# A two-part network on one core: transposed inputs, modulation in column tiles, and three projections woven among its sets

## What is computed

```python
mod = silu(c) @ w_ada[l] + b_ada[l]          # c: one vector of 1024; w_ada: 1024 x 3072
mod_c = silu(c_ctx) @ w_ada[l] + b_ada[l]
shift, scale, gate = split(mod, 3); shift_c, scale_c, gate_c = split(mod_c, 3)
h = rms_norm(x, norm_g[l]) * (1.0 + scale) + shift              # x: 512 x 1024
hc = rms_norm(ctx, norm_g[l]) * (1.0 + scale_c) + shift_c       # ctx: 256 x 1024
# then a = (h @ w_in[:, :512]) * sigmoid(h @ w_in[:, 512:1024]), a convolution over 31 taps, and the rest
```

## Time and profile before

| | |
|---|---|
| Time, median of 3 runs | 3198.05 us (3197.98 to 3198.81) |
| Profiled execution: span | 3200.0 us |
| TensorE busy | 3079.6 us, 96% |
| VectorE busy | 1861.0 us, 58% |
| ScalarE busy | 1308.2 us, 41% |
| GpSimd busy | 344.1 us, 11% |
| DMA | 251.53 MB, mean 79 GB/s |

### The profile page before, as it was taken

The page is one execution under the profiler, slowest core; times in us unless marked ns, Lnnn a source line. Parts: engine busy times, 40 slices in busy tenths (PEclk is TensorE's granted clock), DMA queues, the critical chain, the costliest instruction groups (busy, mean ns, idle before and its releaser), DMA issues.

```text
span 3200.0 us, 37158 instructions
## 1 busy us (share of the span) xinstructions
PE 3079.6 (96%) x14848; PEld 2424.0 (76%) x14848; DVE 1861.0 (58%) x2906; ACT 1308.2 (41%) x2017; POOL 344.1 (11%) x241
## 2 busy tenths in 40 slices
PE   8999999999999999999999999999999989999998
PEld 5877877877788676668667777788888866788887
DVE  5877695455435767673533786666535672466632
ACT  3345534244532344632444464322225567422222
POOL 0011131210000001101220020000003210000000
PEclk9999999999999999999999999999999999999999
DMA  5222132320012322223101232323332310223332
GB/s 209 67 66 73 47 115 77 109 84 26 21 34 76 106 83 74 65 85 101 40 30 50 88 96 80 99 92 94 98 95 89 116 37 1 73 93 94 97 93 73
DMA packets 78733, 251.53 MB, mean 79 GB/s; under 512 B 9120, under 2 KB 11168, under 8 KB 78560
## 3 DMA queue, kind: packets, MB, share of 16 engines
q1 hardware_dynamic: 72672, 227.91, 22.5%
q0 software_dynamic: 5024, 18.09, 1.8%
q10 hardware_dynamic: 864, 3.15, 0.2%
HBM read 247.01 MB, written 2.10 MB: 78 GB/s over the span
## 4 chain that ended last, share of the span: by engine, by line
PE 45%; DVE 3%; ACT 3%; issue 1%; DVEq 0%; ACTq 0%
PE PS L1145 31%; PE PS L1783 3%; PE PS L2800 3%; PE PS L2901 1%; PE PS L1907 1%; PE PS L2878 1%; PE PS L2879 1%; PE PS L2860 0%; PE PS L2861 0%; PE PS L2822 0%; ACT WH L1094 0%; PE PS L2531 0%; ACT L1970 0%; DVE PS L3049 0%; PE PS L2870 0%
## 5 line engine op out<-in xcount | busy, mean ns | idle before, releaser
L1104 DVE TENSOR_TENSOR WL<-RAW,WH 128x1024 fp32r<-128x1024 f32 (+2 forms) x372 | 432.3, 1163 | 513.0 <-ACT WH L1094 512.4
L1094 ACT ACTIVATE WH<-RAW 128x1024 fp32r<-128x1024 f32 (+4 forms) x425 | 407.5, 965 | 430.7 <-PE PS L1145 333.9
L1783 PE MATMUL PS<-Hh,WH 128*128 128x512 f32 x1376 | 516.1, 375 | 14.3 <-DVE WL L1104 6.5
L1783 PE MATMUL PS<-Hh,WL 128*128 128x512 f32 x1376 | 489.2, 356 | 0.0
L1783 PE MATMUL PS<-Hl,WH 128*128 128x512 f32 x1376 | 488.9, 355 | 0.0
L1783 PEld LDWEIGHTS PS<-Hh,WH 128*128 128x128 f32 x1376 | 260.9, 190 | 76.8 <-issue 23.3
L1145 PE MATMUL PS<-XH,WH 128*128 128x512 f32 x768 | 306.1, 399 | 0.0
L1145 PE MATMUL PS<-XH,WL 128*128 128x512 f32 x768 | 304.5, 396 | 0.0
L1145 PE MATMUL PS<-XL,WH 128*128 128x512 f32 x768 | 304.4, 396 | 0.0
L1783 PEld LDWEIGHTS PS<-Hl,WH 128*128 128x128 f32 x1376 | 260.6, 189 | 44.6 <-issue 7.2
L1783 PEld LDWEIGHTS PS<-Hh,WL 128*128 128x128 f32 x1376 | 261.5, 190 | 38.2
(11 more groups left out here) (404 smaller groups left out, 5759.4 us busy)
## 6 DMA issues: line engine op xcount, KB each, us to landing
RAW<-in_w_in SPq DMA_DIRECT2D x124, 512.0 KB, 3.6
RAW<-in_ffn_in SPq DMA_DIRECT2D x96, 512.0 KB, 3.5
RAW<-in_ffn_out SPq DMA_DIRECT2D x48, 512.0 KB, 3.5
RAW<-in_w_ada SPq DMA_DIRECT2D x32, 384.0 KB, 3.6
RAW<-in_nsa_in SPq DMA_DIRECT2D x21, 512.0 KB, 3.3
RAW<-in_lru_in SPq DMA_DIRECT2D x20, 512.0 KB, 3.5
MW<-in_w_ada SPq DMA_DIRECT2D x32, 256.0 KB, 9.6
BS<-in_bs POOLq DMA_DIRECT2D x16, 512.0 KB, 3.9
```

What stands on the lines that cost most here:

```text
L1094: act.activation(WH[half[j]][:, 0:n], RAW[j % NRAW][:, 0:n], ACT.Copy).then_inc(*did("act_whi", ("whi", j)))
L1104: dve.tensor_tensor(WL[half[j]][:, 0:n], RAW[j % NRAW][:, 0:n], WH[half[j]][:, 0:n].bitcast(F32), ALU.subtract).then_inc(*did("dve_wlo", ( ...
L1783: mm = pe.matmul(ps[:, c:c + w_], wt[:, 128 * k:128 * k + 128], x[:, a:a + w_], start=(k == 0 and q == 0), stop=(k == n - 1 and q == 2))
```

## The change

x and the context come transposed from memory in the layout of `X` and `XC2`, so that transposes, copies and `XT` go; they are loaded on SP's queue ahead of the constants. Squares are taken elementwise (ScalarE for x, VectorE for the context), summed over the partitions by full-precision matmuls with ones, and the root is taken on all 768 columns with the helper that later norms use (`act_rsqrt`, `dve_rsqrt`: two halves of 384 columns). A piece of the modulation becomes four matmuls of 128 columns, one into each group of 32 PSUM partitions (a set's 512 results then stand in 4 x 2 partitions by 128 columns, whose other partitions are cleared once), and its turn one matmul with 8 picked columns of the identity. Pieces 0 to 7 run before the first projection. The first three projections (`OPEN`) are opened together: for each set their blocks 2c and 2c+1, with the pieces of the next set between them and its turn at the end. Their weights are loaded early, and GpSimd makes the remainder for the third.

```diff
+AHEAD = ((0, 0), (0, 1), (1, 0))
+OPEN = (("cb", 0, 0), ("ca", 0, 0), ("cb", 0, 1))
 ...
         self.pairs.take("mod0")
-        self.pairs.take("modt0")
-        for i in range(6):
-            self.pairs.take(("x", i))
-            self.pairs.release(("x", i), ("x", i))
         self.pairs.take("roots0")
+        self.rsqrt("r0", "roots0")
+        self.win(("cb", 0, 0), 0, 512)
+        self.win(("ca", 0, 0), 0, 0)
+        self.win(("cb", 0, 1), 0, 640, 2)
         self.rms("in")
-        self.pairs.release("roots0", ("hx", "in", 7, 1))
-        self.pairs.release("mod0", ("row0", 2), ("row0", 3))
-        self.pairs.release("modt0", ("ab0", 2), ("ab0", 3))
+        self.tmp.release(("r0", "y"), ("hx", "in", 7, 0), ("hx", "in", 7, 1))
+        self.pairs.release("mod0", ("sh0", 3), ("ab0", 3), ("row0", 2), ("row0", 3))
 ...
         def sp_begin(sp):
             sp.dma_start(SMA[:, :], t["sm"][:, 0:SM_1]).then_inc(*did("q_sm", ("sm",), by=16))
+            for i in range(4):
+                sp.dma_start(X[:, 2 * i:2 * i + 2, :], t["x"][:, 2 * i:2 * i + 2, :]).then_inc(*did(f"q_x{i}", ("x0", i), by=16))
+            for i in range(2):
+                sp.dma_start(XC2[:, 4 * i:4 * i + 4, :], t["ctx"][:, 4 * i:4 * i + 4, :]).then_inc(*did(f"q_x{4 + i}", ("c0", i), by=16))
 ...
-                if i == 27:
-                    sp_loads(sp, 1)
+                if i == 7:
+                    sp_loads(sp, 2)
 
         def pool_begin(pool):
             pool.memset(EPSC[:, :], EPS).then_inc(*did("pool_set", ("eps",), ("turn", 0)))
+            pool_split(pool, [P.wj[("cb", 0, 1), 0]])
 ...
         def rows0(c):
-            return pairs.of("mod0")[:, 512 * (c % 2):512 * (c % 2) + 512]
+            return pairs.of("mod0")[:, 512 * (c % 2):512 * (c % 2) + 128]
 
         def turned0(c):
-            return pairs.of("modt0")[:, 512 * (c % 2):512 * (c % 2) + 8]
+            return pairs.of("mod0")[:, 512 * (c % 2) + 256:512 * (c % 2) + 264]
 
         def pe_begin(pe):
-            for i in range(6):
-                pe_turn(pe, i)
-                if 1 <= i < 5:
-                    pe_piece(pe, 2 * i - 2)
-                    pe_piece(pe, 2 * i - 1)
-            for i in range(8, 32):
+            ps = pairs.of("roots0")
+            for i in range(4):
+                for w in due("pe", ("sqx0", i), ("co",), pairs.after["roots0"]):
+                    pe.wait_ge(*w)
+                for k in (2 * i, 2 * i + 1):
+                    pe.matmul(ps[:, 0:S], ones, SQX[:, k, :], start=(k == 0), stop=(k == 7))
+            for i in range(2):
+                for w in due("pe", ("sqc0", i)):
+                    pe.wait_ge(*w)
+                for k in range(4 * i, 4 * i + 4):
+                    mm = pe.matmul(ps[:, S:NT], ones, SQC[:, k, :], start=(k == 0), stop=(k == 7))
+            mm.then_inc(*did("pe_sq", ("roots",)))
+            for i in range(8):
                 pe_piece(pe, i)
-                if i in (9, 17, 25):
-                    pe_turn0(pe, i // 8 - 1)
-                if i == 18:
-                    ps = pairs.of("roots0")
-                    for w in due("pe", ("dg",), ("co",), pairs.after["roots0"]):
-                        pe.wait_ge(*w)
-                    for a0, n, c in R768:
-                        mm = pe.matmul(ps[:, c:c + n], ones, DG[:, a0:a0 + n], start=True, stop=True)
-                    mm.then_inc(*did("pe_sq", ("roots",)))
-        def pe_turn(pe, i):
-            ps = pairs.of(("x", i))
-            for w in due("pe", ("xt", i), ("co",), pairs.after["x", i]):
+            pe_turn0(pe, 0)
+            for c in range(4):
+                n = 0
+                steps = [(name, k) for name in OPEN for k in (2 * c, 2 * c + 1)] if c in (0, 3) else [(name, k) for k in (2 * c, 2 * c + 1) for name in OPEN]
+                for name, k in steps:
+                    pe_open(pe, name, k)
+                    n += 1
+                    for i in PIECES[n] if c < 3 else ():
+                        pe_piece(pe, 8 * c + 8 + i)
+                if c < 3:
+                    pe_turn0(pe, c + 1)
+        PIECES = ((), (), (0,), (1, 2), (3, 4), (5, 6), (7,))
+        def pe_open(pe, name, k):
+            ps, j = pairs.of(name), P.wj[name, 0]
+            hi, lo = WH[half[j]], WL[half[j]]
+            xh, xl = hsrc(0)(k)
+            for w in due("pe", ("wlo", j), pairs.after[name], ("hl", "in", k)):
                 pe.wait_ge(*w)
-            for k in range(8):
-                mm = pe.transpose(ps[:, 128 * k:128 * k + 128], XT[i][:, 128 * k:128 * k + 128], ident)
-            mm.then_inc(*did("pe_x", ("xp", i)))
+            for a, n, c in R768:
+                for q, (wt, x) in enumerate(((hi, xh), (hi, xl), (lo, xh))):
+                    mm = pe.matmul(ps[:, c:c + n], wt[:, 128 * k:128 * k + 128], x[:, a:a + n], start=(k == 0 and q == 0), stop=(k == 7 and q == 2))
+            if k == 7:
+                mm.then_inc(*did("pe_lin", ("wfree", j), ("lin", name)))
 
         def pe_piece(pe, i):
             c, k = divmod(i, 8)
-            for w in due("pe", ("mw", i), ("cs",), ("row0", c - 2) if c >= 2 else pairs.after["mod0"]):
+            for w in due("pe", ("mw", i), ("cs",), ("row0", c - 2) if c >= 2 else [("mz",), pairs.after["mod0"]]):
                 pe.wait_ge(*w)
-            pe.matmul(rows0(c)[0:2, :], CS[:, 2 * k:2 * k + 2], MW[i % NMOD][:, :], start=(k == 0), stop=(k == 7)).then_inc(*did("pe_mod", ("mm0", i)))
+            for g in range(4):
+                mm = pe.matmul(rows0(c)[32 * g:32 * g + 2, :], CS[:, 2 * k:2 * k + 2], MW[i % NMOD][:, 128 * g:128 * g + 128], start=(k == 0), stop=(k == 7))
+            mm.then_inc(*did("pe_mod", ("mm0", i)))
 
         def pe_turn0(pe, c):
-            for w in due("pe", ("row0", c), ("co",), ("ab0", c - 2) if c >= 2 else pairs.after["modt0"]):
+            for w in due("pe", ("row0", c), ("co",), ("sh0", c - 2) if c >= 2 else None, ("ab0", c - 2) if c >= 2 else None):
 ...
+            pick = ident.rearrange("p (g n) -> p g n", g=4)[:, :, 0:2]
+            pe.matmul(turned0(c).rearrange("p (g q) -> p g q", g=4), ROW[:, c % 2, :], pick, start=True, stop=True).then_inc(*did("pe_modt", ("turn0", c)))
 ...
+            for i in range(4):
+                for w in due("act", ("x0", i)):
                     act.wait_ge(*w)
-                act.activation(XQ[:, :], XT[i][:, :], ACT.Square, accum_out=NM[:, i:i + 1]).then_inc(*did("act_sq", ("xsum", i)))
+                act.activation(SQX[:, 2 * i:2 * i + 2, :], X[:, 2 * i:2 * i + 2, :], ACT.Square).then_inc(*did("act_sq", ("sqx0", i)))
+            act_rsqrt(act, "r0", NT, load=False)
             act_row0(act, 0)
-            for w in due("act", ("root0", 0)):
-                act.wait_ge(*w)
-            act.activation(NM[:, 16:22], NM[:, 8:14], ACT.Ln).then_inc(*did("act_rs", ("root0", 1)))
-            for w in due("act", ("root0", 1)):
-                act.wait_ge(*w)
-            act.activation(NM[:, 16:22], NM[:, 16:22], ACT.Exp, scale=-0.5).then_inc(*did("act_rs", ("root0", 2)))
-            act_row0(act, 1)
-            act_rms(act, "in", HH[0], lambda k, q: MODS[0][:, k, q:q + 1], (2, 1))
+            act_split(act, 0)
+            act_high0(act, 0)
+            act_split(act, 1)
+            act_high0(act, 1)
+            act_split(act, 2)
+            for c in range(1, 4):
+                act_row0(act, c)
+                act_high0(act, 2 * c)
+                act_high0(act, 2 * c + 1)
 ...
+            for i in range(2):
+                for w in due("dve", pairs.after["mod0"]):
+                    dve.wait_ge(*w)
+                dve.memset(rows0(i), 0.0).then_inc(*did("dve_mz", ("mz",)))
 ...
+                xc = XC2[:, 4 * i:4 * i + 4, :]
+                dve.tensor_tensor(SQC[:, 4 * i:4 * i + 4, :], xc, xc, ALU.mult).then_inc(*did("dve_sq", ("sqc0", i)))
+            dve_rsqrt(dve, "r0", pairs.of("roots0"), NT, 1.0 / 1024, ("roots",))
             dve_turn0(dve, 0)
-            for w in due("dve", ("root0", 2)):
-                dve.wait_ge(*w)
-            dve.scalar_tensor_tensor(NM[:, 24:30], NM[:, 16:22], -0.5, NM[:, 16:22], ALU.mult, ALU.mult).then_inc(*did("dve_rs", ("root0", 3)))
-            for w in due("dve", ("root0", 3)):
-                dve.wait_ge(*w)
-            dve.tensor_tensor(NM[:, 24:30], NM[:, 24:30], NM[:, 8:14], ALU.mult).then_inc(*did("dve_rs", ("root0", 4)))
-            for w in due("dve", ("root0", 4)):
-                dve.wait_ge(*w)
-            dve.scalar_tensor_tensor(NM[:, 16:22], NM[:, 24:30], 1.5, NM[:, 16:22], ALU.add, ALU.mult).then_inc(*did("dve_rs", ("root0", 5)))
-            for i in range(6):
-                for w in due("dve", ("root0", 5), ("co",)):
-                    dve.wait_ge(*w)
-                dve.tensor_scalar(DG[:, 128 * i:128 * i + 128], ident, NM[:, 16 + i:17 + i], None, ALU.mult).then_inc(*did("dve_rs", ("dg",)))
-            dve_turn0(dve, 1)
```

(18 more changed lines are left out.)

97 lines of the change are left out of this document (43 added, 54 removed).

## The result

| | before | changed |
|---|---|---|
| Median of the runs | 3198.43 us | 3231.5 us (3226.03 to 3235.17) |
| Ratio to before | | 1.0092, 95% interval 1.0079 to 1.0105 |
| Span of the profiled execution | 3200.0 us | 3224.2 us |
| Repeated later, ratio to before | | 1.0097, 1.0083 to 1.0110 (r0_again) |

The sign and the range (3204 to 3235) were right; the 3219 of the forecast is 12.5 us too low, and it lies under every run.

The account below looks back on a forecast made before the run. TensorE was taken as the bound: third projection 18.1 us later (92.3 against 74.2) plus a 3.0 us norm stall made a span of 3221.1 us, less 2.0 for the median: 3219 us. Own range 3212 to 3227, wider range 3204 to 3235.

Parts of the forecast that it names:

- Start: Before the first projection: constants land at 12.7 us, sums ready at 24.6, first block at 34.8.
- The second block: Set 0: needs one more remainder and low part after the first block, so it starts at 37.0 us.
- costs nothing: GpSimd's remainder for the third projection: wanted only after several groups of set 0, so no time was counted.
- Set 0 behind its second block: First set from 37.0 us: five blocks 5.3 us and pieces 3.2, plus 0.9 for the clock.
- The 0.9 us of clock: TensorE at half clock after the wait before set 0, partly hidden by the second block's wait; bounds 0 and 2.7.
- The sets: First three projections: pieces 3.2 us a set, three TensorE waits of 4.8 us between sets, 2.0 us of clock each.
- Behind it: After the third projection: AP cleared late, VectorE's conv work late, a stall of 3.0 us at the first norm.
- Later VectorE has slack, and I count nothing: After the first norm: no further loss was counted for the rest of the program.
- The clock did not stay up: Rival at the waits before and between sets: full clock throughout, minus 6.9 us, 3212 us; chance 0.12.
- the constants did not overtake: Rival at the start: constants overtake the big loads, sums start 6 us earlier, 3213 us; chance 0.07.
- tiles ran side by side: Rival in the modulation pieces: tiles run serially, each piece 0.86 us, 3237 us; chance 0.08.
- the last rival: Between sets: modulation chain hidden behind a set's blocks, waits and their clock loss gone, 3199 us; chance 0.12.

Follow-up runs that it names:

- r0_again: The changed kernel unedited, measured once more as the control: 3232.8 us, ratio to before 1.0097.
- r1_turn_early: Changed kernel with all eight pieces of the next set behind a set's first block and the turn behind its second: 3203.97 us, ratio to before 1.0007.
- r10_vector_remainder: Changed kernel with the third projection's first remainder back on VectorE instead of GpSimd: 3228.49 us, ratio to before 1.0086.
- r2_clear_early: Changed kernel with GpSimd clearing AP behind the last turn, not behind the three projections: 3223.6 us.

## Why the prediction was right, and where its sizes were off

- **What bounds it** held: nearly all of the loss is TensorE time before the third projection's end. Forecast 92.3 us, +18.1; measured 96.6, +22.5. The 4.3 us are 1.6 of start, 2.1 of the second block and 1.2 behind it in set 0, less some 0.5 in the rest.
- **Start.** Constants at 14.01 us, forecast 12.7, at the upper bound of 14. Sums 12.4 us, forecast 11.9. Root and VectorE chain to the first block: 10.0 us, forecast 10.2. First block at 36.4, forecast 34.8.
- **The second block** was the mis-sized step: "The second needs one more remainder and low part: 37.0 us", 2.2 us behind the first. It came 4.3 us behind, at 40.66, because GpSimd's remainder, of which I wrote that it "costs nothing", held VectorE's low part for 2.1 us. I priced GpSimd's result and not its company. The Trainium skill has this (SBUF — State Buffer, Who interferes with whom): a VectorE instruction with two SBUF inputs contends with a GpSimd instruction that reads SBUF, and the lock on the shared port pair is an exclusive one. Here the trace agrees: the low part that was 2.84 us long ends some 0.5 us behind GpSimd's remainder, and the pair before it, without GpSimd beside it, took 1.14 us together. This one term is half of the 4.3 us by which the third projection came later than forecast.
- **Set 0 behind its second block** took 10.6 us (40.66 to 51.23), forecast 9.4. The 0.9 us of clock was too little: the second and third block ran at half clock, which cost some 2 us.
- **The sets.** Waits 4.7, 4.7 and 4.8 us, forecast 4.8 each, and r1_turn_early shows their cause. Clock behind them 5.5 us together, forecast 6.0; that this is no fixed price shows r10_vector_remainder, where it was 2.0 more. Between blocks, a group of one piece took 0.42 us and one of two 0.64 (59.44 to 59.86, 61.03 to 61.67), 2.8 a set, forecast 3.2. Sets 1 and 2 without their waits 11.0 and 11.5 us, forecast 11.6; set 3, 8.7, forecast 8.4.
- **Behind it.** The stall at the norm grew by 2.5 us, forecast 3.0; another 0.7 us is a wait for the first product of gate and value that I had not counted. By the marks it is 3.7 us (22.5 to 26.2), and r2_clear_early takes it all away.
- **Sum.** The span was forecast at 3221.1 and measured at 3224.2 us; the median at 3219 and 3231.5. The 12.5 us are 3.1 of span, 5.5 by which the profiled run was the fastest of its four, and 3.9 of an offset: I set the median 2.1 below the span, from one profiled execution of before and other runs of it, while the changed kernel's times stand 1.8 above their spans. Behind the 5.5 is the sentence "Later VectorE has slack, and I count nothing". It held for VectorE, but in the control's profile 1.7 us more are lost by the mark of 1116.1 and 2.5 behind 2544.1, and its stretches below full clock cost 22.7 us, not the 14.1 of the first profile. The kernel before has such stretches too (17.5 us), and I took them for the same in both. The measured median lies outside the forecast's own 3212 to 3227. Only the wider range holds it, and that had been widened for other things, the clock and the constants, so that it held was in part luck.
- **Rivals.** The clock did not stay up; the constants did not overtake; tiles ran side by side; the waits did not vanish. But r1_turn_early is the world of the last rival, 3204 us, and I had said 3199 for it: clock and norm term included it comes within 5 us.

## What to carry to other kernels

When a chain of small steps feeds a busy engine, ask what is still queued on that engine behind the step that starts the chain. Here eight pieces took 1.9 us instead of 7.0 and the kernel became some 30 us slower, and putting the start of a chain four blocks earlier gave 29 us back. And before work is moved to an idle engine, look at what its neighbour does at that moment. A shift of 2 us at the start of a long program can be given or taken by the clock behind short waits much later, so small gains are judged at a mark near the change as well as by the total.
